# Second pair of prompt tiles through all experts densely, in a one-core hybrid decoder step

## The reference, cut to what matters

```python
q = (h @ w_peer_q).reshape(T, 8, 2, 128)           # h: normed rows, 8 heads, two halves
s = einsum('thpc,hpkc->thpk', q, sub_keys)         # 128 keys per half
s1, i1 = top_k(s[:, :, 0], 16)
s2, i2 = top_k(s[:, :, 1], 16)
top_s, top_c = top_k(s1[..., :, None] + s2[..., None, :], 16)   # 16 of 256 pairs
idx = e1 * 128 + e2                                # 16384 experts
g = softmax(top_s)
a = einsum('td,tkd->tk', h, expert_u[idx])         # 8*16 = 128 experts per token
out = einsum('tk,tkd->td', g * gelu(a), expert_v[idx])
```

## Time and profile before

| what | value |
|---|---|
| median of 3 runs | 2293.55 us (2290.17 to 2297.17) |
| the profiled execution's own time, by its span | 2297.1 us |
| TensorE busy | 1633.7 us (71%), mean granted clock 0.805 |
| VectorE busy | 1469.6 us (64%) |
| ScalarE, POOL busy | 857.2 us, 761.1 us |
| bytes moved | 752.49 MB, of which 570.46 MB by the gathers' queue |

### The profile page before, as it was taken

One profiled execution on the slowest core, in us unless ns is written; L12 is line 12 of the kernel. 1 busy time (PEld: TensorE's weight loads), 2 busy tenths in 40 slices (PEclk: granted clock), 3 DMA queues, 4 the chain that ended last, 5 costly groups with the idle time before them and its releaser, 6 DMA issues.

```text
span 2297.1 us, 33413 instructions
## 1 busy us (share of the span) xinstructions
PE 1633.7 (71%) x11544; PEld 742.3 (32%) x11544; DVE 1469.6 (64%) x3591; ACT 857.2 (37%) x2426; POOL 761.1 (33%) x713
## 2 busy tenths in 40 slices
PE   7999999997798977777778989884344343444344
PEld 3556654453343433334443433331000000000000
DVE  2587764124558687878887767336676765676774
ACT  2132233011545434545546543333333332333332
POOL 1254100001232344333433332333354443444443
PEclk9999999998899989899898999995555555555555
DMA  5333555647798989899999999999999999999998
GB/s 185 130 111 124 194 194 200 258 178 275 275 402 334 371 332 357 312 376 371 377 361 361 362 384 410 393 378 387 391 387 405 406 404 372 392 393 406 404 392 362
DMA packets 126884, 752.49 MB, mean 328 GB/s; under 512 B 16468, under 2 KB 40652, under 8 KB 46956
## 3 DMA queue, kind: packets, MB, share of 16 engines
q0 software_dynamic: 78336, 570.46, 63.2%
q1 hardware_dynamic: 48380, 179.90, 21.0%
HBM read 732.61 MB, written 18.54 MB: 327 GB/s over the span
## 4 chain that ended last, share of the span: by engine, by line
PE 32%; DMA 29%; DVE 24%; issue 9%; ACT 4%; POOL 2%; SPq 0%; DVEq 0%; POOLq 0%; ACTq 0%
DMA ring<-in_expert_uv,pick 27%; PE z L1156 19%; DVE ring L1894 6%; PE acc L1310 4%; PE z L1162 2%; PE o L1191 1%; DMA sx<-in_x_prompt 1%; PE o L1244 1%; DVE ti L1795 1%; DVE ti L1798 1%; DVE cand L1836 1%; DVE e L1837 1%; PE s L1208 1%; DVE cand L1834 1%; DVE tv L1797 1%
## 5 line engine op out<-in xcount | busy, mean ns | idle before, releaser
L1088 POOL DMA_INDIRECT ring<-in_expert_uv,pick x544 | 627.2, 1153 | 968.3 <-PE acc L1310 878.7
L1894 DVE CUSTOM_DVE_ANT_0 ring<-ring,rep 128x1024 f32<-128x1024 f32 x544 | 659.9, 1224 | 383.6 <-DMA ring<-in_expert_uv,pick 349.8
L1310 PE MATMUL acc<-ring,fold 128*32 128x256 f32 x4352 | 463.7, 517 | 490.7 <-ACT fold L1483 488.2
L1156 PE MATMUL z<-wts,hT 128*128 128x384 f32 (+1 forms) x1408 | 613.5, 573 | 7.6 <-ACT hT L1492 4.1
L1480 ACT ACTIVATE gel<-dots 128x1 f32<-128x1 f32 x544 | 109.7, 202 | 800.3 <-DVE dots L1894 796.8
L1310 PEld LDWEIGHTS acc<-ring,fold 128*32 128x32 f32 x4352 | 106.2, 126 | 814.3 <-ACT fold L1483 741.9
L1156 PEld LDWEIGHTS z<-wts,hT 128*128 128x128 f32 x1408 | 260.3, 199 | 261.0 <-issue 195.8
L1156 PE MATMUL z<-wts,yT 128*128 128x512 f32 x384 | 192.5, 637 | 13.3 <-ACT yT L1673 7.0
L1483 ACT ACTIVATE fold<-by_pick,gel 128x32 f32<-128x32 f32 x544 | 174.8, 321 | 17.9
L1476 ACT ACTIVATE by_pick<-cst,pick 128x32 f32<-128x32 f32 x544 | 167.0, 307 | 0.0
L1787 DVE SCALAR_TENSOR_TENSOR yT<-uT,vec,yT 128x256 f32<-128x256 f32 x240 | 107.8, 502 | 2.3
(11 more groups left out here) (248 smaller groups left out, 1740.9 us busy)
## 6 DMA issues: line engine op xcount, KB each, us to landing
wts<-in_w_qkv SPq DMA_DIRECT2D x24, 1536.0 KB, 8.0
wts<-in_w_glu SPq DMA_DIRECT2D x8, 2048.0 KB, 11.3
wts<-in_w_gate SPq DMA_DIRECT2D x8, 2048.0 KB, 12.3
wts<-in_w_wq SPq DMA_DIRECT2D x8, 2048.0 KB, 11.3
ring<-in_k_cache SPq DMA_DIRECT2D x8, 1536.0 KB, 9.3
ring<-in_v_cache SPq DMA_DIRECT2D x8, 1536.0 KB, 8.2
rep<-x_h SPq DMA_DIRECT2D x68, 128.0 KB, 9.1
ring<-in_expert_uv,pick POOLq DMA_INDIRECT x544, 11.5
```

The source lines that it names most:

```text
L1088: eng.indirect_dma_start(ring[:, i % RING, :], None, a["expert_uv"], bass.IndirectOffsetOnAxis(picks(i, 0).bitcast(U32), 0)).then_inc(row_ ...
L1156: mm = eng.matmul(bank[:, 0:w], of[:, k, :], rows[:, k, :], start=(k == 0), stop=(k == depth - 1))
L1310: mm = eng.matmul(acc[b][SUB * c:SUB * (c + 1), col:col + 256], fold[:, i % 4, :], ring[:, i % RING, D + 256 * c:D + 256 * (c + 1)], start ...
L1894: eng.tensor_tensor_reduce(u, u, rep[:, j, :], 1.0, 0.0, ALU.mult, ALU.add, dots[:, i % 4:i % 4 + 1]).then_inc(dot_ready, 1)
```

## The change

Tiles 0, 1 and the sample keep their gathered steps: 288 instead of 544. For tiles 2 and 3 together (256 tokens) all 16384 experts are computed. The u rows come transposed as 64 units of 1 MB (256 experts each: two values of the second key times all 128 of the first), the v rows as 64 units of 1 MB, streamed through 4 slots that share the memory of `wts`. New tasks:

- EU, 64 times: TensorE 16 matmuls (128x128 stationary, 256 moving columns) into a bank of 128 experts x 2 x 256 tokens; ScalarE Gelu of 128x512 into `stash`.
- IH, 16 times: the item of one tile and head, all in one piece on VectorE, giving key 1, key 2 and gate of each of a head's 16 picks (`named`); EX: three transposes a tile, so that picks lie on partitions and tokens along the row.
- OH and EG, 128 times (64 for each half of the second key): VectorE builds for four tokens a one-hot of key 1 times gate (4 instructions of 128x128) and a one-hot of key 2 (one of 128x4x64); TensorE multiplies them (4 matmuls of 128x128 by 64 columns), which gives the gates laid out by expert; VectorE multiplies them into the stash (128x256, from PSUM).
- EV, 64 times: TensorE 8 matmuls (128x128 by 512 columns) that add up y in the four banks of `zb` and `sbk`.
- EY: VectorE adds y to the residual, SP stores.

In ticks: 4 IH fall beside the last `w_peer_q` multiplications; then, from `first`, EU 0 to 31 one a tick with the other 12 IH every third tick; EX; 64 ticks of EG; 32 ticks with EV u and EU 32+u; 64 ticks of EG; 32 of EV; EY. The steps are marked up to 160 until `first`, to 244 until the first 64 EG are through, and to 288 at the end. The items of tiles 0, 1 and NT come every 6 steps instead of every 16 and 32.

```diff
-STEP_TILES = (0, 1, NT, 2, 3)
+STEP_TILES = (0, 1, NT)
+DENSE = (2, 3)
+EUNITS = KEYS // 2
+SLOTS = KEYS // 2
+UHALF = SLOTS // 2
+GSLOTS = 2 * P // 4
+STREAMS = 4
+STREAM = [("EU", u) for u in range(UHALF)] + [v for u in range(UHALF) for v in (("EV", u), ("EU", UHALF + u))] + [("EV", UHALF + u) for u in range(UHALF)]
...
+           "EU": 3.5, "EV": 3.5, "EG": 1.5, "IH": 11.0}
...
+    def dense(first):
+        at = ends["SC", 2, 0] + 1
+        for t in DENSE:
+            for h in range(PH):
+                at = max(at, ends["SC", t, h // 2] + 1)
+                put(at, ("IH", t, h))
+                at += 8 if at < first else 3
+            put(max(at, first), ("EX", t))
+        for u in range(UHALF):
+            put(first + u, ("EU", u))
+        at = max(first + UHALF, at + 1)
+        for half in range(2):
+            put(at, ("OH", GSLOTS * half))
+            for s in range(GSLOTS):
+                at += 1
+                if s + 1 < GSLOTS:
+                    put(at, ("OH", GSLOTS * half + s + 1))
+                put(at, ("EG", GSLOTS * half + s))
+            at += 1
+            ends["weigh", half] = at
+            for u in range(UHALF):
+                put(at, ("EV", UHALF * half + u))
+                if half == 0:
+                    put(at, ("EU", UHALF + u))
+                at += 1
+        for t in DENSE:
+            put(at, ("EY", t))
...
+            now = dense(now + 5)
...
-    lo, hi = marks[ENDS[0] - 1], BASE[2] - LAG
+    lo = marks[ENDS[0] - 1]
+    for first, last, hi in ((ENDS[0], ENDS["dense"], EARLY), (ENDS["dense"], ENDS["weigh", 0], MIDDLE), (ENDS["weigh", 0], len(TICKS) - 6, STEPS)):
+EARLY, MIDDLE = 160, 244
...
+            def load_stream(s):
+                kind, u = STREAM[s]
+                if s < STREAMS:
+                    eng.wait_ge(z_ready, last_use(len(UNITS) - 2 + s // 2) + 1)
+                else:
+                    before = STREAM[s - STREAMS]
+                    if before[0] == "EU":
+                        eng.wait_ge(db_ready, DB.no[before] + 1)
+                    else:
+                        eng.wait_ge(weighed, before[1] + 1)
+                eng.dma_start(stream[:, s % STREAMS, :], a["expert_ut" if kind == "EU" else "expert_vt"][u]).then_inc(stream_in[s % STREAMS], 16)
...
+            def expert_products(u):
+                bank = dense_bank_free(("EU", u))
+                rows = stream_use(("EU", u))
+                for x in range(2):
+                    for c in range(DC):
+                        mm = eng.matmul(bank[:, 2 * P * x:2 * P * (x + 1)], rows[:, x, P * c:P * (c + 1)], yT[:, c, :], start=(c == 0), stop=(c == DC - 1))
...
+            def scatter_picks(s):
+                eng.wait_ge(hot_ready, s + 1)
+                for i in range(4):
+                    mm = eng.matmul(bank[:, SLOTS * i:SLOTS * (i + 1)], hot_a[:, s % 2, i, :], hot_b[:, s % 2, i, :], start=True, stop=True)
...
+            def expert_sums(u):
+                freed(eng, DB, db_free, ("EG", GSLOTS * (u // UHALF + 1) - 1))
+                for x in range(2):
+                    n = 2 * u + x
+                    for t in range(2):
+                        for half in range(2):
+                            mm = eng.matmul(y_bank[t][half][:, :], stash[:, n % SLOTS, P * t:P * (t + 1)], rows[:, x, 512 * half:512 * (half + 1)],
+                                            start=(n == 0), stop=(n == KEYS - 1))
...
+            def one_hots(s):
+                for i in range(4):
+                    eng.tensor_scalar(hot_a[:, s % 2, i, :], iota, by[:, 0, i:i + 1], by[:, 2, i:i + 1], ALU.is_equal, ALU.mult)
+                eng.tensor_tensor(hot_b[:, s % 2, :, :], iota[:, SLOTS * half:SLOTS * (half + 1)].unsqueeze(1).to_broadcast([P, 4, SLOTS]),
+                                  by[:, 1, :].unsqueeze(2).to_broadcast([P, 4, SLOTS]), ALU.is_equal).then_inc(hot_ready, 1)
+            def weigh_experts(s):
+                eng.wait_ge(db_ready, DB.no["EG", s] + 1)
+                to = stash[:, :, P * t + 4 * g:P * t + 4 * g + 4].rearrange("p n t -> p t n")
+                eng.tensor_tensor(to, to, dense_bank[DB.bank(("EG", s))][:, 0:4 * SLOTS].rearrange("p (t n) -> p t n", t=4), ALU.mult)
...
+    out["expert_ut"] = x["expert_u"][0].reshape(KEYS, EUNITS, 2, DC, P).transpose(1, 4, 2, 3, 0).reshape(EUNITS, P, -1)
+    out["expert_vt"] = x["expert_v"][0].reshape(KEYS, EUNITS, 2 * D).transpose(1, 0, 2)
```

More of the change, by code:

```diff
@@ L236, in inputs @@
         put(at + 3, ("XT", t, 1))
+    def dense(first):
[9 more added lines that the diff above has]
+        at = max(first + UHALF, at + 1)
+        ends["dense"] = first
+        for half in range(2):
[14 more added lines that the diff above has]
+            put(at, ("EY", t))
+        return at + 1
     for p in range(2):
@@ L414, in step_marks @@
         marks[n] = min(16, int(early[n - START - 7] / 3.2))
-    lo, hi = marks[ENDS[0] - 1], BASE[2] - LAG
-    rest = np.cumsum(cost[ENDS[0]:])
-    for n in range(ENDS[0], len(TICKS)):
-        marks[n] = lo + int((hi - lo) * rest[n - ENDS[0]] / rest[-1] + 1e-9)
+    lo = marks[ENDS[0] - 1]
+    for first, last, hi in ((ENDS[0], ENDS["dense"], EARLY), (ENDS["dense"], ENDS["weigh", 0], MIDDLE), (ENDS["weigh", 0], len(TICKS) - 6, STEPS)):
+        rest = np.cumsum(cost[first:last])
+        for n in range(first, last):
+            marks[n] = lo + int((hi - lo) * rest[n - first] / rest[-1] + 1e-9)
+        lo = hi
+    for n in range(last, len(TICKS)):
+        marks[n] = STEPS
     return marks
+EARLY, MIDDLE = 160, 244
 MARK = step_marks()
 def item_list():
[L428 to L433, removed]
+    out, first = [(-1, 0, 0)], [(0, h) for h in range(1, PH)]
+    rest = [(t, h) for t in (1, NT) for h in range(PH)]
+    while first or rest:
+        at = 6 * len(out) - 6
+        due = first and (at >= 16 * first[0][1] - 22 or not rest)
+        out.append((at, *(first if due else rest).pop(0)))
+    return out
 ITEMS = item_list()
@@ L442 @@
             PARTS.setdefault(_at + _p, []).append((_q, _p))
-SCORES_AT = {ITEMS[q - 1][0] + 2 if q > 2 and (t, h) != (2, 0) else max(at - 3, 0): q for q, (at, t, h) in enumerate(ITEMS) if at >= 0}
+SCORES_AT = {ITEMS[q - 1][0] + 2 if q > 2 else max(at - 3, 0): q for q, (at, t, h) in enumerate(ITEMS) if at >= 0}
 def place_picks():
@@ L461 @@
 TAIL_PICKS = place_picks()
+assert not TAIL_PICKS and all(v[0] != "P" for tick in TICKS[ENDS["SC", 2, 0] + 1:] for v in tick)
 READ_BY_V, READ_BY_A = 0, 1
@@ L528, with dense_uses @@
 ZB, SB, TB, OB = bank_uses()
+def dense_uses():
+    keys = [v for tick in TICKS for v in tick if v[0] in ("EX", "EU", "EG")]
+    return Uses(keys, [READ_BY_V if v[0] == "EG" else READ_BY_A for v in keys], 2)
+DB = dense_uses()
 UNIT_WIDTH = {"glu": DC * 512, "qkv": DC * QW, "gate": DC * 512, "cp": DC * 512, "ap": 4 * 512, "wo": DC * 512, "wq": DC * 512}
@@ L2075, in _ @@
                         signal(eng.tensor_scalar(one, one, -1.0, None, ALU.mult), dm_ready, bt + 1)
+                    elif v[0] == "IH":
+                        dense_item(*v[1:])
+                    elif v[0] == "OH":
+                        one_hots(v[1])
+                    elif v[0] == "EG":
+                        weigh_experts(v[1])
+                    elif v[0] == "EY":
+                        t = v[1]
+                        eng.wait_ge(weighed, EUNITS)
+                        eng.wait_ge(x1_in, 32)
+                        for half in range(2):
+                            ins = eng.tensor_tensor(x1y[:, t % 2, 512 * half:512 * (half + 1)], x1y[:, t % 2, 512 * half:512 * (half + 1)], y_bank[t % 2][half][:, :], ALU.add)
+                        ins.then_inc(dense_y, 1)
                     elif v[0] == "DE":
```

151 lines of the change are left out of this document (135 added, 16 removed).

## The result

The changed kernel takes 2765.22 us (median of four runs, 2763.29 to 2766.61), the kernel before on the same chip 2295.36 (2290.17 to 2298.71): 1.2053 times as long, 95% interval 1.2032 to 1.2075. The forecast was 2685, its range 2540 to 2830. The profiled execution has a span of 2764.5 us and a time of 2766.37.

The account below looks back on a forecast made before the run. The prediction took TensorE to bound the changed kernel, with VectorE pacing the gate stretches and transfers hidden. Its terms, 645 + 727 + 15 + 283 + 154 + 480 + 135 + 231 + 15, gave 2685 us, range 2540 to 2830.

Parts of the forecast that it names:

- Kind and sign: Whole kernel: slower, because 128 dense units make 896 us that cannot lie beside other TensorE work; slower had chance 0.96.
- the chain rows: Profile rows of 16-instruction chains, 6.97 us at 512 columns and 3.65 at 256, pricing a dense unit at 7.0 us.
- the mixed stretch: EV with EU 32 to 63: 463 us of TensorE work plus half of the idle share, 480 us.
- the rival of late streams and half clock: Dense part: half clock adds about 80 us in the EG stretches, late streams lengthen unit stretches; about 2835, chance 0.14.
- First stretch of units: EU 0 to 31 with 59 steps: TensorE 263 us, with 0.93 busy 283 us.
- uncovered: EU 0 to 31: up to 330 us if banks and load lead did not cover the new ScalarE and SP waits.
- Second phase: From 645 us to `first`: TensorE-bound, 677 us of work, 727 with idle time, bounds 677 to 837; units' start adds 15.
- 0.93 busy: TensorE's busy share up to 540 us, used to turn 677 us of second-phase work into 727.
- Two of the signs named: Signs of being right: TensorE 0.9 busy or more from 645 us to `first`, and `first` near 1370.
- Hidden room: TensorE's busy time hides room: at full clock the second phase's 583 us become 534; total 2514, chance 0.09.
- Gates: The two EG stretches: VectorE sets the pace at 1.9 us against TensorE's 1.05, giving 154 and 135 us.
- Not slower: Rival on a dense unit's price: at 4.0 us or less the kernel is no slower than 2297; chance 0.04.

Follow-up runs that it names:

- e2: The changed kernel with half of each dense unit's multiplications left out, the streams kept: 2335.96 us, one run.
- e1: The changed kernel with the item (IH) ranked ahead of the dense unit within a tick: 2709.24 us, ratio to before 1.1806.
- e6: e1 with thirty steps moved earlier, so the second phase carries 174 instead of 144: 2734.66 us, ratio to before 1.1926.
- e11: e10 with thirty steps moved later, out of the second phase, and gathered tiles' items every 5 steps instead of 6: 2187.61 us, ratio to before 0.9545.
- e4: The changed kernel with the gates' product written to contiguous stash elements, so gates land on wrong activations: 2750.0 us, ratio to before 1.1981.
- e5: e1 with two overwritten 256-column products put ahead of each EG's four gate products: 2704.41 us, one run.
- e9: e1 with dense units in 16 bits, the stash kept in 32 bits and cast per unit on ScalarE: 2273.99 us, ratio to before 0.9915.
- e10: e9 with only the planner's costs changed, moving steps from the units' stretches into the gate stretches: 2192.47 us, ratio to before 0.9560.
- e3: The changed kernel with the gates' four products done twice in each EG: 2930.57 us, one run.

## Why the prediction was right, point by point

**Kind and sign.** Right. The 128 units cannot lie beside other TensorE work: their instructions hold 246 + 226 + 230 + 226 = 928 us of it, against 896 forecast from the chain rows, and e2 shows that the time follows their price. Some 20 of the 32 us more are the lower clock of the first stretch. In the mixed stretch and the last one TensorE is full (464 of 464, 231 of 232), and they came out 16 below and 1 above the forecast; the 17 us of idle time added to the mixed one did not come. Its 64 units and 23 gathers are 91 MB, 232 us at 393 GB/s, and not 88 and 224, but hidden either way.

By the number alone the rival of late streams and half clock (2835) lies as near to 2765 as the forecast (2685). What tells them apart is the stretches: its half clock came, its late streams did not.

**First stretch of units: the mis-sized term.** The prediction listed the right wait, "ScalarE's Gelu stands behind steps that wait for VectorE", but in one direction only, and let "two banks and three loads of lead cover both". What it left out is the reverse: VectorE's item waits for ScalarE's exponential, which the order within a tick puts behind the Gelu of that tick's unit, and so behind a unit's multiplications. Two banks don't help, since the queue is in order. 342 us instead of 283, beyond even the "uncovered" 330; e1 removes it and gives 286. By e1 the gaps cost TensorE clock as well as time. The late streams of the rival did not come: the loads landed in 4.8 us (median), and TensorE waited for none of them in that stretch.

**Second phase.** Its work was nearly right: TensorE busy 666 us against 677, a step's `acc` 98/144 = 0.68 us (98.1 us of `acc` in 1156 instructions there) against 0.66. The idle time was not: 768 - 666 = 102 us, where 50 and 15 were forecast; the start of the units holds only 5 of them (TensorE was busy for 4.6 of the 10 us from 1405 to 1415). "0.93 busy", taken from the stretch up to 540, assumed a phase without steps; steps also bring idle time with them (30 us for 30 more in e6, 14 less for 30 fewer in e11). Two of the signs named failed with it: TensorE was 0.87 busy there, not 0.9, and `first` came at 1415, not near 1370. The true figure lay within the bounds given, 677 to 837. VectorE was busy for 548 us against 503, since the four IH of this phase, some 40 us at 10 each, were missing from that sum; it stayed below TensorE.

**Hidden room.** For the most part it did not come: without `acc` TensorE was busy 666 - 98 = 568 us in the second phase, against 583 forecast and 534 in the rival's sum. The Trainium skill (Perfetto Trace Analysis, "Identifying the Most-Contended Engine") warns that busy time is no measure of TensorE's headroom; in this phase the same work shrank by 15 us, 568 beside 583, and not by the rival's 49.

**Gates.** 163 and 142 us against 154 and 135. VectorE was the first bound, as forecast, but its product with the stash cost 0.70 us and not 0.43: the value taken was that of contiguous data (e4 measures 0.42), the bound "at most twice that" held. The one-hots took 0.277 us of busy time each (141.9/512) against 0.26. Together that is 0.34 us a tick, or 22 us in the first stretch, and only 9 came; this was partly luck. Consecutive instructions overlap in the record: VectorE's groups there add up to 175 us (71.0 one-hots, 26.8 compares, 45.2 products, 32.4 dots), while it was busy for 156. So the forecast's sum of single rows was too high where its price of the product was too low. The half clock of the rival came too, at 0.50 and 0.51, and TensorE, forecast half idle, stood close behind with 148 us of 163; it did not add to VectorE's time as the rival had it, and in e5 lifting it, at the price of the fillers, gained nothing.

The Trainium skill (VectorE: DVE Perf Modes, "The perf-mode tier table") gave, by an estimate from it, 0.23 us for such a one-hot. The measured 0.277 decides: of the two values weighed, the row of the two-scalar form was the nearer.

**Not slower.** Its chance of 0.04 was sound, its threshold was not. "4.0 us a unit or less" took all else as fixed, but in e2, at 3.8 us a unit and 2336 us in all, the first stretch of units had become bound by its transfers. With units in 16 bits the kernel came to 0.9% under before (e9); for 4.4% the gathers also had to go to another place (e10).

## What to carry to other kernels

When two engines exchange results inside one tick, follow the wait in both directions: here a 0.3 us instruction ranked behind a wait for another engine's long work cost 56 us of a stretch of 342, and a change of rank brought them back. Before naming the price at which a costlier engine stops being the bound, sum the next resource in the same stretch, and look in which stretch that one is idle: 16-bit units brought the kernel from 2709 to 2274 us, and 82 us more came when the gathers moved to where the DMA engines were half idle. Idle shares do not carry over between stretches with different mixes of work.

## What the runs showed of the hardware

- The granted clock was 0.50 with TensorE busy 148 of 163 us, and 0.50 with it busy 248 of 250 (e3), in both cases on products 64 columns wide; with two 256-column products ahead of each four of these it was 0.98 (e5).
- The same 1024 instructions of 32 EU units kept TensorE busy for 226 us in a stretch with a mean granted clock of 0.99, for 229 at 0.96 (e1) and for 246 at 0.89.
- A product of 128x256 from PSUM into the stash took 0.42 us contiguous, 0.70 with rows 1 KB apart in 32 bits, and 1.43 in the 16-bit stash, where the rows lie 512 B apart.
- An exponential between Gelus on ScalarE cost a table load of 1.28 us and, on the way back, a second one of the same length. The Trainium skill (ScalarE: Activation LUTs, "What ACT_TABLE_LOAD costs") states about 1283 ns for the load, which the trace bears out, and 2.66 us for a switch with a drain; in the timeline above the exponential begins 1.29 us after the load's start, so no second 1.3 us stands there.
